# Splitting the sample tokens' norm off the prompt's, and moving two convolutions forward, in a Mamba-2 mixer fused into its projection

## What is computed

```python
z, xbc, dt = _split(h @ w_in, ODD_SIZES)
xbc = jax.nn.silu(causal_dwconv(xpad, conv_w, conv_b))   # 4 taps over time
xs, bm, cm = _split(xbc, (D_INNER, G_SSM * N_STATE, G_SSM * N_STATE))
# scan over chunks of 128 tokens, 8 groups of 4 heads of 64 channels:
st, y = lax.scan(step, st0, ...)
y = y + d_skip * xs
g = (y * jax.nn.silu(z)).reshape(b, l, G_SSM, D_INNER // G_SSM)
g = g * lax.rsqrt(jnp.mean(g * g, axis=-1, keepdims=True) + EPS)   # per token and group
out = (g.reshape(b, l, D_INNER) * norm_w) @ w_out
```

## Time and profile before

| | |
|---|---|
| median of 3 runs | 3821.55 us (3817.99 to 3832.98) |
| the profiled execution | 3821.55 us, span 3819.9 us |
| PE busy | 3428.7 us (90%), 20568 matmuls |
| DVE busy | 1685.9 us (44%) |
| ACT busy | 1141.6 us (30%) |
| POOL busy | 1161.6 us (30%) |
| mean granted TensorE clock | 0.923 of full speed |

### The profile page before, as it was taken

One profiled execution on the slowest core, in us unless ns is written; L12 is line 12 of the kernel. 1 busy time (PEld: TensorE's weight loads), 2 busy tenths in 40 slices (PEclk: granted clock), 3 DMA queues, 4 the chain that ended last, 5 costly groups with the idle time before them and its releaser, 6 DMA issues. The chain is left out here.

```text
span 3819.9 us, 57131 instructions
## 1 busy us (share of the span) xinstructions
PE 3428.7 (90%) x20568; PEld 3156.7 (83%) x20568; DVE 1685.9 (44%) x2820; ACT 1141.6 (30%) x2097; POOL 1161.6 (30%) x736
## 2 busy tenths in 40 slices
PE   6889987984799999999869999999958999999998
PEld 5539983563599999999758899888848999999998
DVE  3599964673222121212335776777751221212122
ACT  3412211342323131312214555444442231313132
POOL 2004851222032222222215544544544322222222
PEclk8959987986699999999979999999969999999998
DMA  3106555003021111111132222222115111111111
GB/s 119 23 22 97 166 161 184 17 1 115 24 88 49 45 44 50 44 50 44 62 46 78 85 73 90 88 86 89 59 50 177 44 50 45 44 50 44 50 44 67
DMA packets 345875, 263.82 MB, mean 69 GB/s; under 512 B 55926, under 2 KB 311942, under 8 KB 344038
## 3 DMA queue, kind: packets, MB, share of 16 engines
q1 hardware_dynamic: 328102, 228.50, 20.2%
q10 hardware_dynamic: 10496, 15.81, 1.9%
q0 software_dynamic: 7168, 18.08, 1.4%
HBM read 219.43 MB, written 44.76 MB: 69 GB/s over the span
## 5 line engine op out<-in xcount | busy, mean ns | idle before, releaser
L228 POOL TENSOR_TENSOR w_low_sb<-w_loaded_sb,w_high_sb 128x1024 fp32r<-128x1024 f32 (+1 forms) x230 | 558.3, 2428 | 1790.4 <-ACT w_high_sb L222 1779.0
L245 PE MATMUL psum<-act_high_sb,w_high_sb 128*128 128x344 f32 (+1 forms) x2544 | 817.2, 321 | 31.9 <-PEq L186 17.2
L245 PE MATMUL psum<-act_low_sb,w_high_sb 128*128 128x344 f32 (+1 forms) x2544 | 815.4, 321 | 0.0
L245 PE MATMUL psum<-act_high_sb,w_low_sb 128*128 128x344 f32 (+1 forms) x2544 | 815.1, 320 | 0.0
L245 PE MATMUL psum<-second_high_sb,w_high_sb 128*128 128x344 f32 x1704 | 546.3, 321 | 0.0
L245 PE MATMUL psum<-second_low_sb,w_high_sb 128*128 128x344 f32 x1704 | 545.1, 320 | 0.0
L245 PE MATMUL psum<-second_high_sb,w_low_sb 128*128 128x344 f32 x1704 | 545.0, 320 | 0.0
L245 PEld LDWEIGHTS psum<-act_high_sb,w_high_sb 128*128 128x128 f32 (+1 forms) x2544 | 478.6, 188 | 33.8 <-issue 33.3
L245 PEld LDWEIGHTS psum<-act_high_sb,w_low_sb 128*128 128x128 f32 (+1 forms) x2544 | 479.0, 188 | 0.4
L245 PEld LDWEIGHTS psum<-act_low_sb,w_high_sb 128*128 128x128 f32 (+1 forms) x2544 | 478.5, 188 | 0.3
L222 ACT CAST w_high_sb<-w_loaded_sb 128x1024 fp32r<-128x1024 f32 (+1 forms) x230 | 239.8, 1043 | 657.6 <-PE psum L245 601.4
(11 more groups left out here) (409 smaller groups left out, 4934.8 us busy)
## 6 DMA issues: line engine op xcount, KB each, us to landing
w_loaded_sb<-in_w_up SPq DMA_DIRECT2D x64, 512.0 KB, 4.0
w_loaded_sb<-in_w_down SPq DMA_DIRECT2D x64, 512.0 KB, 3.7
w_loaded_sb<-in_w_in_odd SPq DMA_DIRECT2D x48, 512.0 KB, 3.9
key_pages_sb<-in_cache_k SPq DMA_DIRECT2D x64, 256.0 KB, 2.8
ecay_sum_spread_sb<-decay_sum_scratch SPq DMA_DIRECT2D x8, 2048.0 KB, 7.4
w_loaded_sb<-in_w_in_even SPq DMA_DIRECT2D x28, 512.0 KB, 4.1
x_scratch<-x_sb SPq DMA_DIRECT2D x2, 4128.0 KB, 13.3
x_sb<-x_scratch SPq DMA_DIRECT2D x2, 4128.0 KB, 14.9
```

What stands on the lines that cost most here:

```text
L228: self.nc.gpsimd.tensor_tensor(self.wl[:, par, :, 0:width], self.wf[:, par, :, 0:width], self.wh[:, par, :, 0:width].bitcast(F32), ALU.sub ...
L245: ins = nc.tensor.matmul(out, w[:, par, k, 0:width], a[:, k, cols], start=n == 0, stop=n == 3 * KT - 1)
```

## The change

The samples' sums no longer share a tensor with the prompt's. `square_sums_sb` shrinks from 16 to 8 columns; the sample sums go to a row of `sample_small_sb`, with an Ln and an Exp of their own that ACT issues behind the eight scalings of the norm and ahead of silu 0. PE's `sample_sum` moves from slot 8 to a place behind tile (4,0). On DVE `sample_mean` becomes part of `sample_norm`, and the convolutions 0 and 1 of the next group, which stood behind `sample_mean`, are issued at the end of k = 7 and k = 8 of the scan. ACT's silu 1 moves from i = 1 to i = 0, ahead of tile (4,1)'s evacuation.

```diff
-    ss = B.take("square_sums_sb", [P, NBLK + NS])
+    ss = B.take("square_sums_sb", [P, NBLK])
...
-                if k == NBLK:
-                    sample_sum(g)
...
                 if nx is not None:
                     tile(nx, 4, 0)
+                if g is not None:
+                    sample_sum(g)
...
                     act.wait_ge(S["square_sums"], g * 8 + 8)
-                    act.wait_ge(S["sample_mean"], g + 1)
                     nc.scalar.activation(ss[:], ss[:], ACT.Ln, bias=B.eps[:, 0:1], scale=1.0 / 256).then_inc(S["rstd"], 1)
...
                     for n in range(NBLK):
                         nc.scalar.activation(gz[:, n, :], gz[:, n, :], ACT.Copy, scale=ss[:, n:n + 1]).then_inc(S["gated_scaled"], 1)
+                    act.wait_ge(S["sample_mean"], g + 1)
+                    nc.scalar.activation(sml[:, 4, 0:8], sml[:, 4, 0:8], ACT.Ln, bias=B.eps[:, 0:1], scale=1.0 / 256).then_inc(S["rstd"], 1)
+                    act.wait_ge(S["rstd"], g * 4 + 3)
+                    nc.scalar.activation(sml[:, 4, 0:8], sml[:, 4, 0:8], ACT.Exp, scale=-0.5).then_inc(S["rstd"], 1)
...
-                    if nx is not None and i in (1, 3, 5):
+                    if nx is not None and i in (0, 3, 5):
                         if i == 3 and g is not None:
                             act.wait_ge(S["chunk_state_sum"], g * 8 + 8)
-                        silu(nx, {1: 1, 3: 2, 5: 3}[i])
+                        silu(nx, {0: 1, 3: 2, 5: 3}[i])
...
-            def sample_mean(g):
+            def sample_norm(g):
                 dve.wait_ge(S["sample_sum"], g + 1)
                 step(nc.vector.tensor_copy(sml[:, 5, :], B.psum[:, 6, 0:16]))
-                nc.vector.tensor_tensor(ss[:, NBLK:], sml[:, 5, 0:8], sml[:, 5, 8:16], ALU.add).then_inc(S["sample_mean"], 1)
-
-            def sample_norm(g):
-                dve.wait_ge(S["rstd"], g * 2 + 2)
-                step(nc.vector.tensor_tensor(small(2), small(2), ss[:, NBLK:].unsqueeze(1).to_broadcast([P, 2, NS]), ALU.mult))
+                nc.vector.tensor_tensor(sml[:, 4, 0:8], sml[:, 5, 0:8], sml[:, 5, 8:16], ALU.add).then_inc(S["sample_mean"], 1)
+                dve.wait_ge(S["rstd"], g * 4 + 4)
+                step(nc.vector.tensor_tensor(small(2), small(2), sml[:, 4, 0:8].unsqueeze(1).to_broadcast([P, 2, NS]), ALU.mult))
...
                         if k == 5:
                             sample_y(g)
-                    sample_mean(g)
-                    if nx is not None:
-                        for j in range(2):
-                            convolve(nx, j)
+                        if k >= 7 and nx is not None:
+                            convolve(nx, k - 7)
+                if g is not None:
                     sample_norm(g)
```

More of the change, by code:

```diff
@@ L2693, in part @@
                     act.wait_ge(S["square_sums"], g * 8 + 8)
-                    act.wait_ge(S["sample_mean"], g + 1)
                     nc.scalar.activation(ss[:], ss[:], ACT.Ln, bias=B.eps[:, 0:1], scale=1.0 / 256).then_inc(S["rstd"], 1)
-                    act.wait_ge(S["rstd"], g * 2 + 1)
+                    act.wait_ge(S["rstd"], g * 4 + 1)
                     nc.scalar.activation(ss[:], ss[:], ACT.Exp, scale=-0.5).then_inc(S["rstd"], 1)
-                    act.wait_ge(S["rstd"], g * 2 + 2)
+                    act.wait_ge(S["rstd"], g * 4 + 2)
                     act.wait_ge(s_gout, g * 16)
```

## The result

| | before | after |
|---|---|---|
| median | 3809.6 us (3800.2 to 3833.0, 14 runs) | 3844.6 us (3837.3 to 3854.3, 14 runs) |
| ratio | | 1.0090, 95% interval 1.0076 to 1.0104 |
| span of the profiled execution | 3819.9 us | 3860.1 us |
| from the first to the last turn of the convolution rows (L2615), seven rounds | 733.8 us | 764.9 us |

The change costs 34 to 35 us (0.0090 x 3810, and 3844.6 - 3809.6), where 45 were forecast. Both profiled executions ran somewhat longer than the median of their kernel, so the sum is checked against the stretch itself: four matmuls of L2615 end every projection, and from the first start to the last there are seven full rounds (and the 0.3 us or so from the first to the last of one four).

What follows compares the result with a forecast made beforehand. PE was taken to set the round, in step with ACT around the norm. Seven rounds x (3.5 us later start + 2.5 us clock) = 42, plus 3.2 at the end: 45 us on 3821.55, so 3867 us; 8-in-10 range 3844 to 3877.

Steps and rivals of the forecast that it cites:

- the gap on PE: After tile (4,2), PE idles 4.2 us in one piece until it can turn block 2, waiting for ACT's stores.
- the wait in slot 5: PE's wait for DVE's gate, about 4.15 us every round, stays as before.
- The earlier convolutions: Convolutions 0 and 1 issued earlier on DVE buy nothing on ACT; DVE gains 2.46 us of idle time it can spare.
- Their cover: Slack on ACT despite earlier convolutions: 1.5 us ahead of the last square, 1.2 us ahead of the sample mean; cost 0.
- ACT's removed wait: ACT's wait for the sample mean ahead of Ln: no idle time there, so removing it wins nothing.
- rival 1: PE's clock holds through the new 4.2 us gap: 28 us slower in all, 3849 us; chance 15%.
- The clock's term: Behind PE's new gap, mean clock 0.63 over 7.3 us costs 2.5 us a round (1.5 to 3.2).
- The last round: With no tiles to hide behind, ACT's second Ln and Exp shift the mixer's end by 3.2 us.
- rival 2: ACT's new pair needs one table load, not two: gap 2.9 us, 17 us slower, 3839 us; chance 4%.
- 3: Rival: the delay is hidden or given back by misread slack; less than 19 us, near 3832 us; chance 7%.
- 4: Rival: earlier convolutions undo slot 5's DVE-POOL collision, winning 6.6 us a round; 3821 us or less; chance 4%.
- 5: Rival: more than counted, over 3876 us; ACT's slack is missing or another PE step falls behind; chance 6%.

Runs made afterwards that it cites:

- e3: Kernel before with only the samples' Ln and Exp split off and put behind the scalings; ratio 1.0088, round 109.2 us.
- e11: As e8, with a second Ln and Exp on a copy nothing reads and 60 transposes in the fill; ratio 1.0094 to before, round 108.6 us.
- e7: Changed kernel with the samples' Ln and Exp behind the last stores and DVE's sample scaling behind convolution 3; ratio 1.0015 to before, round 105.2 us.
- e4: Changed kernel with 32 transposes nothing reads filling PE's new gap; ratio 1.0068 to before, round 108.0 us.
- e1: Changed kernel with silu 1 put back at i = 1; ratio 1.0091 to before, round 109.2 us.
- e2: Kernel before with the change's convolution order and silu 1 place, but one Ln and Exp for prompt and samples; ratio 1.0027, round 105.7 us.
- e9: Kernel before with POOL's sample-state addition in four and, in slot 4, a weight tile's low half behind two products; ratio 0.9926, round 100.9 us.
- e8: Changed kernel with idle transposes filling both the new gap (32) and slot 5's wait (34); ratio 1.0019 to before, round 105.5 us.

## Why the prediction was right and wrong

**The direction and the place were right.** The pair took 3.14 us (3.16 forecast), the stores begin 4.08 us later (4.12), the gap on PE is 3.9 us (4.2), tile (5,0) starts 3.3 us later (3.5), the clock falls behind the gap in seven of seven rounds, and the wait in slot 5 stays. e3 shows that the second Ln and Exp is enough for the whole loss, e11 that each pair is paid in full when the clock is held, e7 that its place makes it so. The earlier convolutions bought nothing, as forecast: DVE spends what they won in waits of 3.86 and 1.68 us. Their cover was thinner than I had worked out, 0.7 us ahead of the mean in place of 1.2; DVE is idle for 0.52 and 0.46 us in front of the two convolutions, where it was 0.33 and 0.22 before. ACT's removed wait was worth nothing.

**The size was off.** I forecast 45 us and 3867 us; it is 34 to 35 us and 3844.6 us. That lies under my own lower bound of 36 us, which took the clock at 1.5 us a round or more, and at the very edge of the range of times. It is nearer to rival 1's 28 us than to my 45, although the mechanism was mine and not rival 1's. Two things made this:

1. *The clock's term.* The step that failed is "mean clock 0.63 ... so 2.5 us a round". The clock fell as I said, but it came back sooner: the mean behind the new gap is 0.80, and tile (5,0), which took 4.04 us (2343.19 to 2347.23 in the round after the one of the earlier trace rows), takes 2364.38 - 2359.41 = 4.97: 0.9 us. The formula was sound: 7.3 x 0.20 = 1.5 us, less what falls on the wait for block 3. What was wrong was its input, the mean over slot 5's seven windows, put in for another place; two of those windows (0.77) already showed that a gap of the same length can cost much less. The whole of the clock's part is 4.4 - 3.3 = 1.1 us a round: about 1.0 at the new gap (e4), and the rest goes with slot 5 itself, where the mean clock went from 0.63 to 0.62 (7.3 x 0.01 = 0.1 us, an estimate), which I had not counted. With 3.3 for 3.5 and 1.1 for 2.5 the seven rounds make 31 us, as measured. The last round's 4.2 us, for 3.2, holds 1 us more than ACT's pair; e1, e3 and e4 show 3.1 us there, so it isn't the pair's, and its cause stays open.
2. *The time that the sum was added to.* The median of the first three runs, 3821.55 us, lies 12 us above that of fourteen. Of the 22 us by which 3867 missed, 12 are this and 10 the sum's, nearly all of it the clock's term.

**Rivals.** 1 (the clock holds) is refuted by seven windows; even a gap of 3.0 us brings it down (e1, e3, seven rounds of seven each), while one of 1.0 us doesn't in e2 and does in one round of e9. So rival 2, with a gap of 2.9 us, would hardly have kept its clock either. Rival 2's one table load is refuted by the two loads at L2702 and L2704. The page "ScalarE: Activation LUTs" of the Trainium skill, "What ACT_TABLE_LOAD costs", has the load's 1283 ns right; its drain isn't seen here either: the two loads and two activations fill 3.14 us. 3 doesn't hold in any round. 4 didn't happen with this change (the wait in slot 5 is 4.15 to 4.18 us in all rounds), but as a mechanism it is real, and e9 shows what it is worth once POOL's order is changed too: 3.9 us a round, where I had put 6.6. 5 didn't occur.

**What stays open.** e1 and e3 add 3.1 us to ACT's path and the change 4.1, and yet all three have rounds of 109.2 us, each between 109.1 and 109.3, where the kernel before varies from 103.8 to 105.5. In all three the clock is back 6.7 to 7.2 us after the end of tile (4,2), whether the gap ended 3.0, 3.2 or 3.9 us after it; a shorter gap only meant more matmuls at the low clock. So it looks as if PE loses to the clock what it gains by an earlier start. That the return of the clock, not ACT, sets the round's length in these kernels fits with e4, e8 and e11, where it is held and the rounds follow ACT's path again; what fixes the moment of the return wasn't tested, nor why slot 5's clock differs from round to round in the kernel before.

## What to carry to other kernels

Ask of every instruction that is split off not only what it costs but what stands behind it on its engine: a pair of 8-column activations with two table loads cost 0.15% at a place where ACT had idle time, and 0.9% where PE marches in step with ACT. A short wait (here 0.37 us) that recurs in every round is a sign that the chain before it has no slack: with the clock held, 3.1 us more on ACT cost 3.2 us a round. Count a gap on PE with the clock behind it, but give that price the whole spread that the trace shows for such gaps, and room below it, since another place and even another round can differ, and if the gap can't be removed, try filling it with matmuls that nobody reads: in slot 5 that alone was worth 0.6%.

## What the runs showed of the hardware that I had not expected

- The granted clock fell behind gaps of 3.0 us on PE (seven of seven rounds, e1), and once in seven rounds behind waits of 1.05 and 0.22 us (e9). How soon it was back at 1.00 didn't follow from the gap's length: 2.9 to 3.1 us after the end of the 3.9 us gap of the changed kernel, 3.9 to 4.2 after the 3.0 us gap of e1, and 3.6 to 6.8 after the 4.15 us wait of slot 5 in the kernel before.
- Three kernels whose critical path differs by up to 0.96 us a round had the same round, 109.2 us, to 0.1 us, as long as the clock fell in each round.
- POOL's addition of 128x2048 takes 4.77 us whole and 5.82 us in four parts with DVE's instructions between them; DVE's multiply, 0.69 us at its shortest, then takes 1.56 in place of 4.87.
